# Cross-attention and self-attention products one or two steps later, and SSD decay sums made as rows once

## The reference, cut to what matters

```
p = softmax(q k^T / 8 + bias);  o = p v                          # 8 heads
A_cs = cumsum(dt * A)                                            # per SSD head
M[s, l] = exp(A_cs[l] - A_cs[s]) * dt[s] * (B[s] . C[l])  for s <= l
y[l] = sum_s M[s, l] * x[s] + D * x[l];  y = rmsnorm(y * silu(z))
```

## Time and profile before

| | us |
|---|---|
| median of three runs | 1499.75 |
| the profiled execution | 1502.82 |
| its span | 1500.9 |
| TensorE busy | 1164.3 (78%) |
| VectorE busy | 324.1 (22%) |
| ScalarE busy | 200.1 (13%) |
| chain that ended last: TensorE's share | 52% |
| chain that ended last: transfers' share | 38% |
| mean granted TensorE clock | 0.914 of full |

### The profile page before, as it was taken

The page is one execution under the profiler, slowest core; times in us unless marked ns, Lnnn a source line. Parts: engine busy times, 40 slices in busy tenths (PEclk is TensorE's granted clock), DMA queues, the critical chain, the costliest instruction groups (busy, mean ns, idle before and its releaser), DMA issues.

```text
span 1500.9 us, 14530 instructions
## 1 busy us (share of the span) xinstructions
PE 1164.3 (78%) x6002; PEld 577.0 (38%) x6002; DVE 324.1 (22%) x835; ACT 200.1 (13%) x468; POOL 43.7 (3%) x79
## 2 busy tenths in 40 slices
PE   8999998887786775775769999987866666567575
PEld 5775544553232222231326776454422122122121
DVE  1126432232011110110102365222211011011011
ACT  2024302210000000000002251122000000000000
POOL 1110000000000000000001100000000000000000
PEclk9999999989898898997989999999998898898888
DMA  9563345059999999999997353625799999999996
GB/s 370 196 224 112 123 186 187 30 215 416 425 424 428 426 427 425 427 427 425 427 391 285 112 169 125 233 91 195 296 423 428 427 427 426 427 427 427 428 427 253
DMA packets 94356, 477.99 MB, mean 318 GB/s; under 512 B 6390, under 2 KB 15054, under 8 KB 44878
## 3 DMA queue, kind: packets, MB, share of 16 engines
q1 hardware_dynamic: 93367, 475.25, 78.3%
q10 hardware_dynamic: 919, 1.74, 0.3%
HBM read 475.92 MB, written 1.05 MB: 318 GB/s over the span
## 4 chain that ended last, share of the span: by engine, by line
PE 52%; DMA 38%; DVE 5%; ACT 2%; issue 2%; SPq 1%; DVEq 0%; ACTq 0%
PE bank L1400 50%; DMA ring<-exp_w 37%; PE bank L1407 2%; SPq L543 1%; DMA conv_mem<-memT 1%; DMA ring<-w_in 1%; DVE fox_ssd L1154 0%; ACT Y L688 0%; ACT SCO L886 0%; DVE SCO L1005 0%; DVE fox_ssd L1224 0%; ACT fox_ssd L726 0%; ACT H L874 0%; DVE smax L1286 0%; DVE SCO L1136 0%
## 5 line engine op out<-in xcount | busy, mean ns | idle before, releaser
L1400 PE MATMUL bank<-ring,proj_ht 128*32 128x512 f32 (+3 forms) x2496 | 450.7, 666 | 151.7 <-DMA ring<-exp_w 149.7
L1400 PEld LDWEIGHTS bank<-ring,proj_ht 128*32 128x32 f32 (+1 forms) x2496 | 169.0, 141 | 388.9 <-issue 376.5
L1400 PE MATMUL bank<-ring,SCO 128*32 128x512 f32 x928 | 133.4, 712 | 69.7 <-DMA ring<-exp_w 60.7
L1400 PE MATMUL bank<-ring,H 128*128 128x512 f32 x256 | 117.2, 614 | 3.3 <-ACT H L688 1.5
L1014 DVE TENSOR_TENSOR X<-X,bank 128x512 f32<-128x512 f32 x64 | 44.0, 688 | 316.8 <-PE bank L1400 316.8
L1400 PE MATMUL bank<-proj_ht,H 128*128 128x128 f32 x512 | 76.8, 303 | 32.3 <-DVE proj_ht L973 28.3
L1400 PEld LDWEIGHTS bank<-ring,SCO 128*32 128x32 f32 x928 | 36.9, 127 | 150.8 <-issue 140.2
L1400 PEld LDWEIGHTS bank<-proj_ht,H 128*128 128x128 f32 x512 | 67.1, 208 | 71.3 <-DVE proj_ht L973 40.1
L1005 DVE SCALAR_TENSOR_TENSOR SCO<-Y,bank 128x512 f32<-128x512 f32 x16 | 17.1, 1069 | 284.4 <-PE bank L1400 284.4
L1400 PEld LDWEIGHTS bank<-ring,H 128*128 128x128 f32 x256 | 49.3, 197 | 62.3 <-issue 61.0
L1400 PE MATMUL bank<-fox_ssd,proj_ht 128*128 128x512 f32 x128 | 59.1, 604 | 17.8 <-ACT fox_ssd L726 17.8
(11 more groups left out here) (200 smaller groups left out, 847.1 us busy)
## 6 DMA issues: line engine op xcount, KB each, us to landing
ring<-exp_w SPq DMA_DIRECT2D x182, 2048.0 KB, 19.9
ring<-w_in SPq DMA_DIRECT2D x8, 2048.0 KB, 16.0
ring<-xa_wkv SPq DMA_DIRECT2D x4, 2048.0 KB, 9.8
ring<-w_out SPq DMA_DIRECT2D x4, 2048.0 KB, 8.9
ring<-xa_wq SPq DMA_DIRECT2D x4, 2048.0 KB, 9.6
ring<-xa_wo SPq DMA_DIRECT2D x4, 2048.0 KB, 7.8
ahead<-xa_wkv SPq DMA_DIRECT2D x4, 2048.0 KB, 28.1
ring<-w_in SPq DMA_DIRECT2D x6, 1024.0 KB, 12.6
```

What stands on the lines that cost most here:

```text
L1400: return nc.tensor.matmul(dst, lhsT, rhs, start=start, stop=stop)
```

## The change

1. **Cross-attention** (`cross_steps`): scores in step j, `xpT` of head j-2, `xo` of head j-3. Probabilities, their transposes, maxima and sums have four buffers. VectorE divides head j-1 after taking the maximum of head j. The two `out2` products of tile 0 move behind the last scores, to steps 8 and 10, and the residual additions behind the loop.
2. **Self-attention** (`attend`): the value products of two heads run one step later, ahead of the next `pT`. The last pair runs behind `cb`. ScalarE's copies (`copy_o`) move with them.
3. **Decay sums**: VectorE zeroes `DLx` and copies the eight columns into it, so that head pair g stands at columns 32g and 32g+1. One job `cumT` makes the running sums as rows, and VectorE masks them to `sums` (two operations, `take_sums`) in step 0. `spread(g)` is then one product of 512 columns over 32 rows of ones and serves two heads. All four run before the last `pT`, and their banks stay held. A new semaphore `shifted` releases ScalarE.
4. **SSD heads**: `Ms` has five buffers, so head h waits for the products of head h-5. TensorE runs the first chunks of `out1` for tile 0 before the head products, and those for tile 1 behind them. Four banks of `L`, two of `y` and two of `out1` are held at once there.

```diff
-CROSS_BETWEEN = [[("q", 1, 1)], [], [], [("qT", 1, 0), ("qT", 1, 1)], [], [("out2", 0, 0)], [("out2", 1, 0)], [], []]
-L_AHEAD = 2
+CROSS_LAG = 2
+N_MS = 5
...
+def cross_steps():
+
+    steps = []
+    for j in range(len(CROSS) + CROSS_LAG + 1):
+        step = [("xs", *CROSS[j])] if j < len(CROSS) else []
+        step += {0: [("q", 1, 1)], 3: [("qT", 1, 0), ("qT", 1, 1)]}.get(j, [])
+        if 0 <= j - CROSS_LAG < len(CROSS):
+            step += [("xpT", *CROSS[j - CROSS_LAG])]
+        if j > CROSS_LAG:
+            step += [("xo", *CROSS[j - CROSS_LAG - 1])]
+        step += {len(CROSS): [("out2", 0, 0)], len(CROSS) + CROSS_LAG: [("out2", 1, 0)]}.get(j, [])
+        steps.append(step)
+    return steps
...
+        if k >= 3 and k % 2:
+            jobs += [("o", HEADS[k - 2])]
         if k:
             jobs += [("pT", HEADS[k - 1])]
-            if k % 2 == 0:
-                jobs += [("o", HEADS[k - 1])]
-    jobs += [("xsT", t) for t in range(NT)] + [("cb", g) for g in range(2)] + [AFTER_CB[l]]
-    jobs += [("y", t) for t in range(NT)] + [("L", h) for h in range(L_AHEAD, SH)]
-    jobs += [("out1", n, t) for t in range(NT) for n in range(2)]
+    jobs += [("xsT", t) for t in range(NT)] + [("cb", g) for g in range(2)] + [("o", HEADS[-1]), AFTER_CB[l]]
+    jobs += [("out1", 0, 0), ("out1", 1, 0)] + [("y", t) for t in range(NT)] + [("out1", 0, 1), ("out1", 1, 1)]
...
+            if job == ("out1", 0, 1):
+                held -= {place[l, ("L", g)][0] for g in range(SH // 2)}
...
-            if job[0] == "y":
+            if job[0] in ("L", "y", "out1"):
                 held.add(b)
-            if job == ("L", SH - 1):
+            if job == ("ysT", NT - 1):
...
+        Ms = [view(fqt_flat, h * 3 * P, 3 * P) if h < 3 else view(dqt_flat, (h - 3) * 3 * P, 3 * P)
+              for h in range(N_MS)]
+        CB = view(fqt_flat, 9 * P, 2, 3 * P)
+
+        DLx = view(pt[0], 0, NT, 4, 32)
+        sums = view(pt[1], 0, 2, S)
...
+        XP, XPT = view(sq, 0, 4, S), view(Yf, 0, 4, S)
+        xp_max, xp_sum = (b[:, :, :].rearrange("p a b -> p (a b)") for b in (smax, ssum))
...
+                        copy_o(len(HEADS) - 1)
...
-                    act.wait_ge(*copied(l, ("L", h)))
+                    act.wait_ge(shifted, at(shifted, l, h + 1))
...
+                link(v.memset(DLx.rearrange("p t g b -> p (t g b)"), 0.0))
+                v.tensor_copy(DLx[:, :, :, 0:2], DL[:, :, NH:].rearrange("p t (g b) -> p t g b", b=2)
+                              ).then_inc(DLx_ready, 1)
...
+                def take_sums():
+
+                    job = ("cumT",)
+                    dve.wait_ge(*full(l, job))
+                    for b in range(2):
+                        last = v.tensor_scalar(sums[:, b, :], bk(l, job)[:, 0:S], c_("pair")[:, b:b + 1], None,
+                                               ALU.mult)
+                    last.then_inc(read(l, job), 1)
+                    dve.wait_ge(*copied(l, job))
+                    dve.sem_inc(sums_ready, 1)
...
-                    if h >= 2:
-
-                        dve.wait_ge(y_head, at(y_head, l, h - 1))
-                    v.scalar_tensor_tensor(Ms[:, h % 2, 0:S], Ls[l][:, h % 2, 0:S], DTs[:, 0, h:h + 1],
-                                           CB[:, h // 4, 0:S], ALU.mult, ALU.mult)
-                    v.scalar_tensor_tensor(Ms[:, h % 2, S:], Ls[l][:, h % 2, S:], DTs[:, 1, h:h + 1],
+                    if h >= N_MS:
+
+                        dve.wait_ge(y_head, at(y_head, l, h - N_MS + 1))
+                    M = Ms[h % N_MS]
+                    tile0 = v.scalar_tensor_tensor(M[:, 0:S], Ls[l][:, h % 2, 0:S], DTs[:, 0, h:h + 1],
+                                                   CB[:, h // 4, 0:S], ALU.mult, ALU.mult)
+                    if h % 2:
+
+                        tile0.then_inc(read(l, ("L", h // 2)), 1)
...
-                    if j < len(CROSS):
-
-                        dve.wait_ge(*copied(l, job))
-                        normalize(SCO[:, j % 2, 0, :], ssum[:, j % 2, 0:1], xprobs)
-                    if j in (6, 7):
-                        residual("out2", j - 6, 0)
+                    if j:
+                        b = (j - 1) % 4
+                        dve.wait_ge(*copied(l, ("xs", *CROSS[j - 1])))
+                        normalize(XP[:, b, :], xp_sum[:, b:b + 1], xprobs)
+                for n in range(2):
+                    residual("out2", n, 0)
...
+                job = ("cumT",)
+                pe.wait_ge(DLx_ready, at(DLx_ready, l, 1))
+                pe.wait_ge(*free(l, job))
+                d = DLx.rearrange("p t g b -> p t (g b)")
+                mm(bk(l, job)[:, 0:S], d[:, 0, :], tri[:, 0:S], stop=False)
+                mm(bk(l, job)[:, P:S], d[:, 1, :], tri[:, 0:P], start=False).then_inc(filled(l, job), 1)
...
-                def spread(h):
-
-                    job = ("L", h)
+                def spread(g):
+
+                    job, r = ("L", g), slice(32 * g, 32 * g + 32)
                     pe.wait_ge(*free(l, job))
-                    d = [DL[:, t, NH + h:NH + h + 1].to_broadcast([P, P]) for t in range(NT)]
-                    mm(bk(l, job)[:, 0:S], d[0], tri[:, 0:S], stop=False)
-                    mm(bk(l, job)[:, P:S], d[1], tri[:, 0:P], start=False).then_inc(filled(l, job), 1)
+                    mm(bk(l, job)[:, :], ones[r, :], sums.rearrange("p b s -> p (b s)")[r, :]
+                       ).then_inc(filled(l, job), 1)
...
-                        for h in range(L_AHEAD):
-                            spread(h)
+                        pe.wait_ge(sums_ready, at(sums_ready, l, 1))
+                        for g in range(SH // 2):
+                            spread(g)
+                    if k >= 3 and k % 2:
+                        attend(k - 2)
...
+                attend(len(HEADS) - 1)
...
-                for t in range(NT):
-                    pe.wait_ge(*copied(l, ("xsT", t)))
-                    pe.wait_ge(*free(l, ("y", t)))
-                for h in range(SH):
-                    if h + L_AHEAD < SH:
-                        spread(h + L_AHEAD)
-                    pe.wait_ge(M_ready, at(M_ready, l, h + 1))
-                    c = slice(SP_ * h, SP_ * (h + 1))
-                    M = Ms[:, h % 2, :]
-                    y0 = mm(bk(l, ("y", 0))[:, c], M[:, 0:P], XS[:, 0, c])
-                    if h == SH - 1:
-                        y0.then_inc(filled(l, ("y", 0)), 1)
-                    mm(bk(l, ("y", 1))[:, c], M[:, P:S], XS[:, 0, c], stop=False)
-                    y1 = mm(bk(l, ("y", 1))[:, c], M[:, S:], XS[:, 1, c], start=False)
-                    y1.then_inc(filled(l, ("y", 1)) if h == SH - 1 else y_head, 1)
 
                 def out1(n, t, chunks):
 
@@ -1697,9 +1737,24 @@
 
                 for k in (1, 3, 5, 7):
                     pe.wait_ge(*copied(l, ("o", HEADS[k])))
-                for t in range(NT):
-                    for n in range(2):
-                        out1(n, t, range(4))
+                for n in range(2):
+                    out1(n, 0, range(4))
+
+                for t in range(NT):
+                    pe.wait_ge(*copied(l, ("xsT", t)))
+                    pe.wait_ge(*free(l, ("y", t)))
+                for h in range(SH):
+                    pe.wait_ge(M_ready, at(M_ready, l, h + 1))
+                    c = slice(SP_ * h, SP_ * (h + 1))
+                    M = Ms[h % N_MS]
...
+                for n in range(2):
+                    out1(n, 1, range(4))
...
+                for j, step in enumerate(cross_steps()):
+                    for job in step:
+                        if job[0] == "xs":
+                            _, t, h = job
+                            if h == 0:
+                                both_copied("qT", t)
+                            pe.wait_ge(*free(l, job))
+                            for c in (2 * h, 2 * h + 1):
+                                last = mm(bk(l, job)[:, 0:S], QT[:, t, c, :], KT[:, c, :], start=c == 2 * h,
+                                          stop=c == 2 * h + 1)
+                            last.then_inc(filled(l, job), 1)
+                        elif job[0] == "q":
+                            query(1, 1)
+                        elif job == ("qT", 1, 0):
+                            transpose_q(1)
+                        elif job[0] == "xpT":
+                            b = j - CROSS_LAG
+                            pe.wait_ge(xprobs, at(xprobs, l, b + 1))
+                            transposes(l, job, [XP[:, b % 4, m * P:(m + 1) * P] for m in range(2)])
+                        elif job[0] == "xo":
+                            _, t, h = job
+                            b = (j - CROSS_LAG - 1) % 4
+                            pe.wait_ge(*copied(l, ("xpT", t, h)))
+                            pe.wait_ge(*free(l, job))
+                            for i in range(2):
+                                d0 = h * XD + i * P
+                                for m in range(2):
```

(14 more changed lines are left out.)

132 lines of the change are left out of this document (51 added, 81 removed).

## The result

| | before | after |
|---|---|---|
| median (range) of the runs compared, us | 1500.53 (1496.08 to 1502.77, 4 runs) | 1456.94 (1455.06 to 1458.08, 4 runs) |
| profiled execution, its span | 1502.82, 1500.9 | 1456.56, 1454.7 |
| TensorE busy | 1164.3 (78%) | 1142.2 (79%) |
| mean granted TensorE clock | 0.914 | 0.909 |

The ratio is 0.9715, 95% interval 0.9688 to 0.9741: 43.6 us gained, where 27.5 were forecast. So the sign and the places were right and the sizes were not.

A forecast was written before the change was run, and what follows sets the result against it. The expert-weight stream has a fixed length and starts behind TensorE's dense stages, so their savings move the end. Gains of 14.6 us (layer 0) and 12.9 (layer 1), 27.5 off the 1499.75 median, gave 1472.2 us; range 1462 to 1485.

The forecast's parts named there:

- Part 1: Before the SSD, self-attention with `cumT`, late `attend` and new spreads: net gain 0.3 us a layer.
- Part 2: SSD, kv product to `ysT`, the main gain: 21.3 us by TensorE's work; gain 8.8 us in layer 0, 7.1 in layer 1.
- Part 3: Cross-attention: of 8.97 us of waits three remain, in steps 2 to 4, 3.5 us together; gain 5.5 us a layer.
- The late `attend` removes the 1.04 us: Self-attention: the value products' wait for ScalarE's copy goes, 1.04 us in layer 0 and the same assumed in layer 1.
- I take the full price: Self-attention step 8: four spreads over 32 rows cost 0.86 us each, 3.4 us, as if not running concurrently.
- The wait is gone: Self-attention step 8: the last transposes' 2.18 us wait goes, probabilities being ready 1.7 us sooner; step neither gains nor loses.
- 4.5 us from the clock: SSD, `out1`: the clock stays at 2.4 GHz instead of falling to 1.2, worth 3.1 + 1.4 us.
- The clock: Rival: clock falls at thinned SSD heads and cross-attention, leaving 20.5 us gained, 1479.2 us; chance 0.16.
- VectorE as the bound: Rival, SSD: the last `Ms` and work on `Y` run 2.5 us a layer late, 1477.2 us; chance 0.11.
- the stream held: Rival: the expert-weight stream's first loads are held by dense-stage transfers, nothing passes on, 1499.7 us; chance 0.03.
- not as said: Rival: held banks make `attend` or `kv` wait for ScalarE, TensorE idles through the SSD, 1488.2 us; chance 0.05.
- slower: Rival: the clock stays at 1.2 GHz through cross-attention, 1552 us if all its products ran at half speed; chance 0.05.

The follow-up runs named there:

- e5: The kernel before with only self-attention's value products one step later (`attend`, `copy_o`): 1489.46 us, against 1499.80 for the kernel before in that session.
- e6: The kernel before, with TensorE waiting for both copies of `pT` ahead of each pair of value products instead of one by one: 1507.64 us, ratio 1.0056.
- e7: The changed kernel with three of four pairs of self-attention value products pulled apart, one head ahead of the transposes, the other behind: 1462.63 us.
- e4: The changed kernel with both tiles' first `out1` chunks behind the head products, as before; five `Ms` buffers stay: 1473.46 us.
- e8: The changed kernel with two buffers for `Ms` instead of five: 1472.35 us.
- e2: The changed kernel with self-attention's value products early again, behind the `pT` of their second head: 1469.29 us.
- e3: The changed kernel with decay sums the old way, two products for each of eight heads, all in step 8, without `cumT`: 1464.40 us.
- e11: The changed kernel with two of eight chunks of the last kv product or z projection ahead of self-attention's last transposes: 1456.36 us.
- e10: The changed kernel with `qT` behind step 3's probability transposes and value product, and VectorE dividing head 2 before normalizing the queries: 1453.84 us.
- e12: The changed kernel with the edits of e10 and e11 together: 1454.59 us.

## Why the prediction was wrong in size

By the trace, in both layers, start to start:

| step of the prediction | forecast | measured |
|---|---|---|
| Part 1, start of the layer to the end of the kv product | 0.6 | 4.7 + 4.1 = 8.8 |
| Part 2, from there to `ysT` | 15.9 | 10.0 + 8.3 = 18.3 |
| Part 3, cross-attention | 11.0 | 7.5 + 8.5 = 16.0 |
| sum | 27.5 | 43.1 |

- **Part 1 failed, and it is half of the miss.** "The late `attend` removes the 1.04 us" priced the wait that the trace showed and not the products beside it. The signs were in the trace: the pair's first half is x4 with 0.86 us and a wait of 1.04 behind it, and the last pair is x8 with 1.50 us, less than twice 0.86. I took 0.86 for the price of one half wherever it stood. The runs show 0.8 to 0.9 us for a pair whose halves can start together (e5, the first three pairs of e6, the last of e7) and 1.4 to 1.7 where the second half's operand lands while the first runs. In layer 0 that is 1.89 us at the first pair with its wait, 0.94 and 0.84 at the next two, and 0.62 at the last: 4.3 us, and 4.1 in layer 1, where the forecast had 1.04 each. This is 6.3 us of the 8.2 that Part 1 is off.
- **"I take the full price" failed for the spreads.** 3.4 us were put down, and the row says 1.14 (32 of the 128 rows each, x8). I had the other case at hand, with 3.4 us better over both layers, but took "every row with fewer than 128 rows that I read is no cheaper" for evidence, though none of those rows had neighbours in other rows of the array. The Trainium skill (TensorE: Matmul & The Clock Gate, Part 3, Packing small matmuls) was right: four such products in 1.14 us where four full ones take 3.4 is 3.0 times, beside its 3.07. The Trainium skill (TensorEngine Tiling (Array Packing), Tiling Modes) also has two tiles of 128 by 64 that work in parallel. That is the shape of the value products; 0.81 us for a pair beside 0.79 for one half agrees with it, and the forecast did not weigh it.
- **"The wait is gone" failed in step 8.** With spreads that short nothing covers VectorE, and 1.14 and 1.23 us stay. The net gain of the step is still 3.65 - 2.29 = 1.4 us in layer 0, and 3.27 - 2.36 = 0.9 in layer 1, instead of nothing.
- **Part 2 held.** No wait, the clock up, VectorE never the releaser. The remainder is the term of 0.78 us a head: it is 5.3 / 8 = 0.66. The 0.78 was half of a row's length, which counts to its modelled end, and not a distance from start to start; in the changed kernel the row of two heads is 1.50 us long and the next one starts 1.34 behind it. The 0.3 us of uncovered work on `Y` did not show. The "4.5 us from the clock" came: `out1` takes 6.87 + 6.93 = 13.8 us in each layer, where it took 16.9 and 15.2. In e4 and e8 the clock falls again and part of them is lost.
- **Part 3 held in its mechanism**: 2.50 us before `qT` where 2.6 were forecast (its own two times give 2.5). Of the other two waits of 0.5 and 0.4 us, one is 0.30 and the other absent. So 8.97 - 2.80 = 6.2 us of waits went in layer 0, where 5.5 were forecast. The other 1.3 us are the error of Part 1 once more, products priced at nothing because only waits were counted. One head before:

```profile
267.91 1.03 PE L1400 MATMUL bank<-keys_values,proj_ht 128*128 128x256 f32 x4
...
270.51 1.16 PE L1400 MATMUL bank<-Y,keys_values 128*128 128x128 f32 x8 [1.35 <-ACT Y L688]
271.50 1.03 PE L1400 MATMUL bank<-keys_values,proj_ht 128*128 128x256 f32 x4
```

It takes 3.59 us, 2.24 without its wait, and a head now takes 1.98. In layer 1 the clock's fall also got shorter by about 1 us. Together the two layers are 2 and 3 us over the forecast.
- **The rivals.** The clock: where that rival had it, it fell once, for 3 us in layer 1's cross-attention, which has such a fall before the change too; not where the SSD was thinned. It fell in a place that nobody had named, the router of layer 0, and took 1.5 us. So one of the prediction's own signs of being wrong, 0.5 where it was 1.0, did come, and no step of the forecast hung on it. VectorE as the bound, the stream held, not as said, slower: none came. The range was too narrow downward, for it moved three known unknowns and none of the prices that I had read from rows with gaps in them.

## What to carry to other kernels

Before pricing a move by the wait that it removes, price the instructions on both sides of it in their new neighbourhood: in this kernel two products that use different columns of the array cost as much as one when both could start together, and up to twice that when the second one's operand landed while the first ran. A wait that a trace shows behind such a product is only what is left of it. Read such a price from a row that has no gap and the same neighbour, and if there is none, keep both ends in the range. An order and the buffers that let another engine run ahead for it (e4 and e8) are one change; test them together.

## What the runs showed of the hardware

- Two value products of 64 columns each: 0.81 us together, 0.79 for one alone (e7), 1.74 at the second pair of layer 0 of e2, where the second half's copy lands while the first runs. No wait shows in the last case, for the first half's own time hides it; e6 makes it visible, 0.97 us at the second pair.
- Four products over 32 rows each, 512 columns: 1.14 us together.
- The clock behind one and the same wait of 2.50 us before `qT`: in the eight kernels that have the wait whole, cross is longer by 1.2 us or more in 12 of 16 layers (layer 1 always, layer 0 in e3, e7, e8 and e11) and not in the other four. In e10 and e12, where the waits stand apart, none above 1.13 us, it never is. In layer 0 of e3 and e11 the windows behind the wait show 0.50 for 2 us, in layer 0 of the changed kernel and of e2 they show 1.00. So within one program the clock falls behind this wait in one layer and not in the other, and each fall costs 1.2 to 2.6 us. What decides it no run here shows. The Trainium skill (TensorE: Matmul & The Clock Gate, HAM oscillation) has idle gaps bring the clock down. The direction agrees; four of 16 stretches behind the same gap kept 1.00.
